# An encoder kernel's opening: the first modulation in three pieces instead of two, and the first units by pieces

## The reference

```python
mods = (jax.nn.silu(c) @ ada_w[i] + ada_b[i]).reshape(bsz, 9, D_MODEL)
h = _modulate(x, mods, 0)          # x * (1 + mods[:, 1]) + mods[:, 0]
y = _swiglu(h, ffn_w_in[i, 0], ffn_w_out[i, 0])
x = _layer_norm(ALPHA * x + 0.5 * mods[:, 2, None, :] * y, ln_g[i, 0], ln_b[i, 0], dtype)
```

## Time and profile before

| | before |
|---|---|
| median of 3 runs | 2230.73 us (2228.91 to 2231.63) |
| profiled execution, its own time | 2232.09 us |
| its span | 2230.4 us |
| TensorE busy | 2157.1 us, 97% of the span |
| VectorE busy | 1240.9 us, 56% |
| ScalarE busy | 818.1 us, 37% |
| mean granted TensorE clock | 0.985 |
| loads | 265.30 MB, mean 119 GB/s |

### The profile page before, as it was taken

The page is one execution under the profiler, slowest core; times in us unless marked ns, Lnnn a source line. Parts: engine busy times, 40 slices in busy tenths (PEclk is TensorE's granted clock), DMA queues, the critical chain, the costliest instruction groups (busy, mean ns, idle before and its releaser), DMA issues.

```text
span 2230.4 us, 30506 instructions
## 1 busy us (share of the span) xinstructions
PE 2157.1 (97%) x10535; PEld 1793.0 (80%) x10535; DVE 1240.9 (56%) x1920; ACT 818.1 (37%) x1114; POOL 234.0 (10%) x229
## 2 busy tenths in 40 slices
PE   2999999999998999999999999999999989999998
PEld 2888888878886888888788888878888878888887
DVE  5666565655567666655644533576676555333345
ACT  4331222455434321222532222376665535322223
POOL 0000000342113000001200000241101122000002
PEclk7999999999999999999999999999999989999999
DMA  7656562333333657643234532332121122323321
GB/s 277 216 175 191 184 191 76 98 103 86 94 107 120 207 169 221 203 123 102 86 96 136 169 98 68 112 95 67 56 75 56 38 67 85 90 85 109 99 71 56
DMA packets 401861, 265.30 MB, mean 119 GB/s; under 512 B 9192, under 2 KB 361864, under 8 KB 401800
## 3 DMA queue, kind: packets, MB, share of 16 engines
q1 hardware_dynamic: 401800, 264.52, 39.4%
HBM read 262.32 MB, written 2.19 MB: 119 GB/s over the span
## 4 chain that ended last, share of the span: by engine, by line
PE 92%; DVE 4%; ACT 2%; issue 1%; DMA 1%; SPq 0%; POOL 0%; DVEq 0%; ACTq 0%
PE ps L1305 25%; PE ps L1307 25%; PE ps L1306 25%; PE ps L1320 2%; PE ps L1321 1%; PE ps L1326 1%; PE ps L1486 1%; DVE w_lo L739 1%; PE ps L1345 1%; PE ps L1393 1%; PE ps L1527 1%; PE ps L1508 1%; PE ps L1429 1%; PE ps L1455 1%; PE ps L1519 1%
## 5 line engine op out<-in xcount | busy, mean ns | idle before, releaser
L739 DVE TENSOR_TENSOR w_lo<-raw,w_hi 128x1024 fp32r<-128x1024 f32 (+2 forms) x384 | 436.1, 1136 | 769.6 <-ACT w_hi L540 768.7
L540 ACT ACTIVATE w_hi<-raw 128x1024 fp32r<-128x1024 f32 (+2 forms) x384 | 371.8, 969 | 1166.3 <-PE ps L1307 1104.6
L1305 PE MATMUL ps<-h_hi,w_hi 128*128 128x512 f32 x1744 | 689.0, 395 | 1.8 <-ACT q_sig L613 1.4
L1307 PE MATMUL ps<-h_hi,w_lo 128*128 128x512 f32 x1744 | 679.5, 390 | 0.0
L1306 PE MATMUL ps<-h_lo,w_hi 128*128 128x512 f32 x1744 | 678.7, 389 | 0.0
L1305 PEld LDWEIGHTS ps<-h_hi,w_hi 128*128 128x128 f32 x1744 | 327.4, 188 | 74.0 <-issue 3.1
L1307 PEld LDWEIGHTS ps<-h_hi,w_lo 128*128 128x128 f32 x1744 | 327.3, 188 | 69.6
L1306 PEld LDWEIGHTS ps<-h_lo,w_hi 128*128 128x128 f32 x1744 | 327.6, 188 | 67.2 <-issue 1.4
L1305 PE MATMUL ps<-g_hi,w_hi 128*128 128x512 f32 x704 | 275.7, 392 | 0.0
L1307 PE MATMUL ps<-g_hi,w_lo 128*128 128x512 f32 x704 | 274.1, 389 | 0.0
L1306 PE MATMUL ps<-g_lo,w_hi 128*128 128x512 f32 x704 | 273.9, 389 | 0.0
(11 more groups left out here) (230 smaller groups left out, 2093.7 us busy)
## 6 DMA issues: line engine op xcount, KB each, us to landing
raw<-in_ffn_w_in_dram SPq DMA_DIRECT2D x176, 512.0 KB, 3.7
ada_raw<-in_ada_w_dram SPq DMA_DIRECT2D x128, 512.0 KB, 4.4
raw<-in_ffn_w_out_dram SPq DMA_DIRECT2D x64, 384.0 KB, 3.3
raw<-in_ffn_w_out_dram SPq DMA_DIRECT2D x64, 320.0 KB, 3.1
raw<-in_hgrn_w_in_dram SPq DMA_DIRECT2D x40, 512.0 KB, 3.7
raw<-in_na_w_qkv_dram SPq DMA_DIRECT2D x24, 512.0 KB, 3.6
boot<-in_ada_w_dram SPq DMA_DIRECT2D x16, 512.0 KB, 8.6
tab<-bias_rows SPq DMA_DIRECT2D x16, 256.0 KB, 3.6
```

The costliest lines, as they stand in the source:

```text
L540: nc.scalar.activation(w_hi[s][:, 0:ph.kt, :], raw[s][:, 0:ph.kt, :], ACT.Copy).then_inc(S.w_hi_done, 1)
L739: nc.vector.tensor_tensor(w_lo[s][:, 0:ph.kt, :], raw[s][:, 0:ph.kt, :], w_hi[s][:, 0:ph.kt, :].bitcast(F32), ALU.subtract).then_inc(S.w_l ...
L1305: nc.tensor.matmul(ps[:, bank, :], w_hi[s][:, k, :], a, start=start and k == 0, stop=False)
L1307: ins = nc.tensor.matmul(ps[:, bank, :], w_lo[s][:, k, :], a, start=False, stop=stop and k == ph.kt - 1)
```

## The change

The first two modulation rows are made in three pieces: the columns of k = 0 to 3, then k = 4, 5, then k = 6, 7. The first piece is summed by VectorE in eight steps as before. For each of the two smaller ones VectorE sums seven of the eight rows of ada_w in steps of 512 columns instead of 1024, and TensorE multiplies the eighth row directly by c_silu, accumulating in the same PSUM columns as the reduction. SyncE's queue is put in another order (c first, x as two halves of the channels, the weight tiles between the pieces, the bias table's first load before ada_raw). ScalarE makes all h_hi of a piece before its h32. VectorE sums part of the next piece before the low parts of the piece in front. TensorE's first four units no longer go over all k at once, but take what each piece makes ready, with filler matmuls in between (`boot_idle`, `boot_busy`). The two columns AG and AB are made later, and the phases' counting constants follow (a third boot slot).

```diff
@@ constants
+BOOT_K0 = [0, 4, 6, 8]
+BOOT_DVE = [8, 7, 7]
+BOOT_BASE = [0, 7, 13]
+BOOT_Q = 3
+BOOT_STEPS = 19
+X_BANK = [4, 5, 3]
...
@@ SyncE
+            def boot_load(q, row):
+                k0, k1 = BOOT_K0[q], BOOT_K0[q + 1]
+                src = ada[0, row, :, 0:2 * D].rearrange("p (m c) -> p m c", m=2)[:, :, k0 * P:k1 * P]
+                if q == 0:
+                    b, dst = row, boot[row][:]
+                else:
+                    b = (q - 1) * 4 + row // 2
+                    dst = boot[b][:, (row % 2) * HM:(row % 2 + 1) * HM]
+                    if row == 0 and q == 1:
+                        sp.wait_ge(S.ada_step, 4)
+                    elif row == 0:
+                        sp.wait_ge(S.acc_out_ready, 1)
+                sp.dma_start(dst.rearrange("p (m c) -> p m c", m=2), src).then_inc(S.boot_loaded[b], 16)
+
+            def x_load(h):
+                c = slice(h * HM, (h + 1) * HM)
+                sp.dma_start(x_tok[:, :, c], x_in[0, :, c].rearrange("(t p) d -> p t d", p=P)).then_inc(S.x_loaded[h], 16)
+
+            sp.dma_start(vrow[40:48, 2, :], c_in.rearrange("b (r p) -> (b r) p", p=P)).then_inc(S.c_in, 16)
+            sp.dma_start(vrow[0:8, 2, :], hgrn_norm_g.rearrange("l (r p) -> (l r) p", p=P)).then_inc(S.c_in, 16)
+            sp.dma_start(vrow[8:40, 2, :], hgrn_lb_logits.rearrange("a l (r p) -> (a l r) p", p=P)).then_inc(S.c_in, 16)
+            for row in range(4):
+                boot_load(0, row)
+            x_load(0)
             sp.dma_start(vrow[0:72, 0, :], ada_b[0].rearrange("(r p) -> r p", p=P)).then_inc(S.small_in, 16)
             sp.dma_start(vrow[0:72, 1, :], ada_b[1].rearrange("(r p) -> r p", p=P)).then_inc(S.small_in, 16)
...
-            for k in range(2 * KT):
-                if k == 14:
-                    sp.wait_ge(S.acc_out_ready, 1)
-                elif k >= 7:
-                    sp.wait_ge(S.ada_step, k - 6 - k // 15)
-                two = ada[0, k % KT, :, 0:2 * D].rearrange("p (m h c) -> p m h c", m=2, h=2)
-                sp.dma_start(boot[k % 7][:].rearrange("p (m c) -> p m c", m=2), two[:, :, k // KT, :]).then_inc(S.boot_loaded[k % 7], 16)
-                if k == 3:
-                    for t in range(T // P):
-                        sp.dma_start(x_tok[:, t, :], x_in[0, t * P:(t + 1) * P, :]).then_inc(S.x_loaded, 16)
-                if k == 11:
-                    load(phases[0], 0, 0)
-            for s in range(1, 4):
-                load(phases[0], 0, s)
+            for row in range(4, 8):
+                boot_load(0, row)
+            load(phases[0], 0, 0)
+            load(phases[0], 0, 1)
+            x_load(1)
+            for row in range(8):
+                boot_load(1, row)
+            load(phases[0], 0, 2)
+            load(phases[0], 0, 3)
+            for row in range(8):
+                boot_load(2, row)
...
@@ ScalarE
-            for s in range(4):
-                convert(phases[0], 0, s)
-            make_h(0)
+            for k in range(4):
+                x_across(k)
+            convert(phases[0], 0, 0)
+            convert(phases[0], 0, 1)
+            boot_h(0)
+            for k in range(4, KT):
+                x_across(k)
+            convert(phases[0], 0, 2)
+            convert(phases[0], 0, 3)
+            boot_h(1)
+            boot_h(2)
...
@@ VectorE
+            boot_steps(0, range(8))
...
-            boot_step(KT)
-            boot_step(KT + 1)
+            convert(phases[0], 0, 0)
             boot_columns(0)
-            for g in range(2, KT):
-                boot_step(KT + g)
-                if g in (4, 5, 6):
-                    low_parts(0, g - 4)
-            convert(phases[0], 0, 0)
+            convert(phases[0], 0, 1)
+            low_parts(0, 0)
+            low_parts(0, 1)
+            boot_steps(1, range(0, 4))
+            low_parts(0, 2)
+            low_parts(0, 3)
+            boot_steps(1, range(4, 7))
+            convert(phases[0], 0, 2)
             boot_columns(1)
-            for k in range(3, KT):
-                low_parts(0, k)
-                if k in (4, 5, 6):
-                    convert(phases[0], 0, k - 3)
+            convert(phases[0], 0, 3)
+            boot_steps(2, range(0, 4))
+            low_parts(0, 4)
+            low_parts(0, 5)
+            boot_steps(2, range(4, 7))
+            col(nc.vector.tensor_scalar(AG[:], vec[:, 0, 72:120].rearrange("p (a b) -> p a b", b=KT), ALPHA, None, ALU.mult))
+            col(nc.vector.tensor_scalar(AB[:], vec[:, 1, 72:120].rearrange("p (a b) -> p a b", b=KT), ALPHA, None, ALU.mult))
+            col(nc.vector.tensor_copy(AG[:, NLN - 1], vec[:, 0, 112:120]))
+            col(nc.vector.tensor_copy(AB[:, NLN - 1], vec[:, 1, 112:120]))
+            boot_columns(2)
+            low_parts(0, 6)
+            low_parts(0, 7)
...
@@ TensorE
+            def reduce_boot(q):
+                k0, n = BOOT_K0[q], BOOT_K0[q + 1] - BOOT_K0[q]
+                column = lambda k: (k // n) * KT + k0 + k % n
+                if q > 0:
+                    b = (q - 1) * 4 + 3
+                    pe.wait_ge(S.boot_loaded[b], 48)
+                    pe.wait_ge(S.norm_done, k0)
+                    for k in range(2 * n):
+                        nc.tensor.matmul(ps[:, 7, column(k):column(k) + 1], boot[b][:, HM + k * P:HM + (k + 1) * P], c_silu[:, KT - 1:KT],
+                                         start=k == 0, stop=False, skip_group_check=True)
+                pe.wait_ge(S.acc_out_ready, q + 1)
+                for k in range(2 * n):
+                    ins = nc.tensor.matmul(ps[:, 7, column(k):column(k) + 1], acc_out[:, k * P:(k + 1) * P], one[:],
...
+            def boot_high(s, ks):
+                pe.wait_ge(S.w_lo_done, s + 1)
+                for k in ks:
+                    pe.wait_ge(S.h_hi_done, k + 1)
+                    nc.tensor.matmul(ps[:, s, :], w_hi[s][:, k, :], h_hi[:, k, :], start=k == 0, stop=False)
+                    nc.tensor.matmul(ps[:, s, :], w_lo[s][:, k, :], h_hi[:, k, :], start=False, stop=False)
+
+            def boot_low(s, ks):
+                for k in ks:
+                    pe.wait_ge(S.h_ready, k + 1)
+                    ins = nc.tensor.matmul(ps[:, s, :], w_hi[s][:, k, :], h_lo[:, k, :], start=False, stop=k == KT - 1)
+                if ks[-1] == KT - 1:
+                    ins.then_inc(S.unit_done, 1)
+
+            def boot_idle(times):
+                for _ in range(times):
+                    nc.tensor.matmul(ps[:, 2, 0:P], ident[:], ident[:], start=True, stop=True)
+
+            def boot_busy(times):
+                for _ in range(times):
+                    nc.tensor.matmul(ps[:, 6, :], w_hi[0][:, 0, :], w_hi[0][:, 0:4, :], start=True, stop=True)
...
+            x_turned(0)
+            boot_idle(12)
             reduce_boot(0)
+            pe.wait_ge(S.vec_done, 2)
+            pe.wait_ge(S.w_hi_done, 1)
+            boot_busy(6)
+            boot_high(0, range(0, 4))
+            boot_high(1, range(0, 4))
+            x_turned(1)
+            for s in range(2):
+                boot_low(s, range(0, 4))
+            boot_busy(4)
             reduce_boot(1)
+            boot_high(2, range(0, 4))
+            for s in range(3):
+                boot_high(s, range(4, 6))
+            pe.wait_ge(S.xt_done, KT)
+            boot_high(3, range(0, 6))
+            boot_low(2, range(0, 4))
+            boot_low(3, range(0, 4))
+            reduce_boot(2)
+            for s in range(4):
+                boot_low(s, range(4, 6))
+            for s in range(4):
+                boot_high(s, range(6, 8))
+                boot_low(s, range(6, 8))
...
-                        if ph.half == 0 and isinstance(i, int):
+                        if ph.half == 0 and isinstance(i, int) and ph.n == 0:
+                            pe.wait_ge(S.pair_free, 2)
+                        elif ph.half == 0 and isinstance(i, int):
```

126 lines of the change are left out of this document (71 added, 55 removed).

## The result

| | before | after |
|---|---|---|
| first measurement, median | 2231.18 us (4 runs) | 2216.19 us (2214.15 to 2218.37, 4 runs) |
| ratio, 95% interval | | 0.9934 [0.992, 0.9947] |
| second measurement, median | 2231.93 us (9 runs) | 2213.41 us (2212.66 to 2216.79, 5 runs) |
| ratio, 95% interval | | 0.9919 [0.9905, 0.9932] |
| profiled execution, its span | 2232.09, 2230.4 us | 2216.05, 2214.3 us |

Faster by 15.0 us in the first measurement and 18.5 in the second; 15.5 was forecast.

What follows compares the result with a forecast made beforehand. TensorE holds 92% of the chain of waits, so time is won only where it stands still, in the opening. Loop opens at 62.3 instead of 80.56 (18.3), less 2.8 for the clock: 15.5 won, 2215 us, range 2208 to 2225.

Steps and rivals of the forecast that it cites:

- Front of the queue: Opening loads: ada_w starts 1.6 us earlier, its fifth row another 2.3; row at 14.3, sum complete 5.5 later at 19.8.
- First half: Columns of k = 0 to 3: reduction done at 21.8, hidden behind VectorE's work to 22.4; first h_hi at 23.1 us.
- First quarter: Columns of k = 4, 5: VectorE's chain ends at 36.3 us, TensorE's branch at 36.1, a tie.
- Second quarter: Columns of k = 6, 7: VectorE's sums end at 45.2, TensorE last at 47.1 us; low part 7 at 51.4.
- Into the loop: First ride loses its cover, stands behind low part 7 until 57.9; 4.4 more, loop opens at 62.3, gain 18.3 us.
- The clock: TensorE idles 5.7 of 6.6 us before the loop; 4 to 7 us at half speed, 2 to 3.5 lost, 2.8 taken.
- The rival that the reduction between the two waits keeps the clock up: At the loop's door: standing still splits into 2.2 and 3.6 us, clock stays up, 18.3 won, 2212.5; chance 0.17.
- The first row: First of two later TensorE idle stretches in the old profile: clock fell after 4.6 us standing, returned after 6.9 of work.
- Edits costed at nothing: Opening fillers (1 to 2 us together if waits go), AG and AB, table load, shorter ada_w pieces: 0.3 inside the roundings.
- the low clock in the opening: TensorE falls to 1.2 GHz in its bursts from 19.8 to 36; half taken, 9 us less won, 2224; chance 0.12.
- its own sum of 14.6: Low clock through the whole opening costs 14.6 of the 18.3 us; part of a slower-than-before case, 2235, chance 0.04.
- The sum: Whole kernel: 18.3 us gained at the loop's door less 2.8 for the clock, 15.5 won; 2215 on the median's scale.

Runs made afterwards that it cites:

- e2_ride_later: Changed kernel with the first ride moved out of the opening into the loop's iterations, the third such phase giving its extra start back; 2213.08 us, ratio 0.991.
- a0_again: The changed kernel unaltered, measured and profiled a second time beside the kernel before; 2213.41 us, ratio 0.9919.
- e4_low_first: Changed kernel with VectorE's low parts of each piece put ahead of all sums of the next piece; 2218.5 us, ratio 0.994.
- e5_no_fillers: Changed kernel without its 22 filler matmuls of the opening (12 boot_idle, 6 + 4 boot_busy); 2216.13 us, ratio 0.9923.
- e8_eighth_on_vector: Changed kernel with the eighth ada_w row of both quarters summed by VectorE again, TensorE's direct products left out; one run, 2217.5 us.
- e1_hold: Changed kernel with 22 filler matmuls on TensorE at the loop's door, eight before the first ride's reduction, fourteen behind; 2213.48 us, ratio 0.9918.

## Why the prediction was right

- *Front of the queue*: row at 14.3, sum at 19.8 forecast; 14.04 and 19.49 measured. Three terms taken whole, none was lost; at x's use (13.77) TensorE had waited for the small rows up to 13.34, and not for x.
- *First half*: h_hi at 23.1, measured 22.70, after w_lo as forecast.
- *First quarter*: 36.3, measured 36.07; the forecast had the branches tie with VectorE last (36.3 and 36.1). VectorE was through at 35.44, 0.9 earlier, and waited 0.63 for TensorE, whose four fillers stood on the path.
- *Second quarter*: 47.1, measured 47.27, TensorE last, as forecast; low part 7 ends at 51.66 (51.4).
- *Into the loop*: ride to 58.02 (57.9), door at 62.42 (62.3). That the ride, costing nothing before, goes onto the path, was the step that could most easily have been missed; e2_ride_later confirms it, together with the loads that stood in line behind it.
- *The clock*: low for 6.16 us of the loop (4 to 7 forecast), 2.84 lost (2.8 taken). a0_again has 5.45 and 2.52, and the three other profiled executions with the ride in the opening and no fillers at the door (e4_low_first, e5_no_fillers, e8_eighth_on_vector) 2.9 to 5.1 us and 1.3 to 2.4 lost, so the range was right and the nearness to 2.8 luck. TensorE stood for 4.4 us ahead of the door (1.82 + 2.56), not 5.7: its products ended 0.65 later than forecast, and the reduction took 1.69 instead of 0.95, since the clock fell within it. The rival that the reduction between the two waits keeps the clock up failed in all five. The first row was read rightly, but it is only the beginning of a wait. TensorE of the kernel before, timeline:

```profile
671.41 0.39 PE L1307 MATMUL ps<-ona_hi,w_lo 128*128 128x512 f32 x1
679.83 1.86 PE L1345 MATMUL ps<-mean_w,zsum 128*128 128x1 f32 x8 [8.04 <-POOL zsum L1182]
...
683.27 0.77 PE L1305 MATMUL ps<-ona_hi,w_hi 128*128 128x512 f32 x1
```

  It stood for 8.04 us, until GpSimd's zsum, and the clock fell 4.65 into that (676.45). The 96 products of these four units are all in the records, 90 ahead of the wait and six from 683.27 on.
- *Edits costed at nothing*: the shorter pieces of ada_w did not hold up the sums; no sum of the two quarters waited for a DMA. "They come within 5 us, ahead of use", said of iteration 1's weights, held by 0.6 us only at w_lo and not at all at g, where ScalarE's branch behind that tile ended 0.1 after VectorE's, and it failed in e1_hold. This cost was on the edge of the path and deserved a range of its own. The fillers, given 1 to 2 us if the waits over them go, cost 0.5 ahead of the second reduction.
- *The rivals*: the low clock in the opening was priced at 9 for half of its case, where half of its own sum of 14.6 is 7.3. e5_no_fillers, where it did come, lost 0.8 by it at the first reduction and nothing behind, since it ended before TensorE became the bound.
- *The sum*: 15.5 forecast for the change, 18.14 - 2.84 = 15.3 in the trace, 15.8 in a0_again's. The profiled execution came out at 16.0 because two later dips, unforeseen, nearly cancelled (+1.9 and -2.8). The prediction had no term for such draws; of its range some 3 us either way belong to them. That the first measured difference (15.0) came within 0.5 of the forecast is luck, too: the second was 18.5.
